# Weight transfers asked for before the row stores land, and the first experts' weight slots refilled by quarters

## What is computed

```python
def hier_moe(u, w_rg, b_rg, w_re, b_re, w_gate, w_up, w_down):
    # top-1 of 4 groups, then top-2 of the 8 experts in that group
    ...
    for e in range(N_EXPERTS):                       # 32
        h = jax.nn.silu(x @ w_gate[e]) * (x @ w_up[e])   # 1024 -> 512
        y = y + cw[:, e:e + 1] * (h @ w_down[e])         # 512 -> 1024
...
h = h + mixer(rmsnorm(h))           # one input projection, short convolution, retention, w_o
h = h + hier_moe(rmsnorm(h))
h = h + (p @ w_ple_proj) * sigmoid(rmsnorm(h) @ w_ple_gate);  y = rmsnorm(h)
```

## Time and profile before

| | |
|---|---|
| median of three runs | 840.43 us |
| the profiled execution | 840.24 us |
| its span | 838.4 us (1.8 us lie around it) |
| TensorE busy | 736.6 us (88%) |
| VectorE, ScalarE, GpSimd busy | 279.1, 180.9, 101.8 us |
| DMA queue q1 | 27248 packets, 237.17 MB, 68.9% of 16 engines' span |
| chain that ended last | TensorE 49%, DMA 34%, VectorE 6% |

### The profile page before, as it was taken

One profiled execution on the slowest core, in us unless ns is written; L12 is line 12 of the kernel. 1 busy time (PEld: TensorE's weight loads), 2 busy tenths in 40 slices (PEclk: granted clock), 3 DMA queues, 4 the chain that ended last, 5 costly groups with the idle time before them and its releaser, 6 DMA issues.

```text
span 838.4 us, 11322 instructions
## 1 busy us (share of the span) xinstructions
PE 736.6 (88%) x4530; PEld 459.6 (55%) x4530; DVE 279.1 (33%) x498; ACT 180.9 (22%) x278; POOL 101.8 (12%) x159
## 2 busy tenths in 40 slices
PE   8999999999999888989999887777777777778996
PEld 7988899989999823333333322222222222226675
DVE  5554578576431632011010100100100100104875
ACT  7242321223331300011111110000000000004576
POOL 0500000000010212211212121121121121110000
PEclk9999999999999989999999999999999999999998
DMA  9541216451763789999999999999999999996301
GB/s 347 227 178 51 75 64 227 176 210 72 295 222 102 281 319 421 418 428 424 425 425 427 424 427 424 426 427 426 426 428 426 428 426 426 426 427 239 151 27 75
DMA packets 36280, 257.30 MB, mean 307 GB/s; under 512 B 7860, under 2 KB 8420, under 8 KB 22792
## 3 DMA queue, kind: packets, MB, share of 16 engines
q1 hardware_dynamic: 27248, 237.17, 68.9%
q0 software_dynamic: 6896, 18.00, 5.7%
q10 hardware_dynamic: 2096, 1.55, 0.6%
HBM read 249.96 MB, written 15.13 MB: 316 GB/s over the span
## 4 chain that ended last, share of the span: by engine, by line
PE 49%; DMA 34%; DVE 6%; ACT 2%; issue 2%; DVEq 0%; SPq 0%; POOLq 0%; ACTq 0%
DMA arena<-in_w_exp 32%; PE ps L1547 19%; PE ps L1739 15%; PE ps L1756 5%; PE ps L1870 3%; PE ps L1590 1%; DVE xh L1410 1%; PE ps L1665 1%; PE ps L1688 1%; PE ps L1655 1%; DMA region_u<-h_rows,index 1%; DVE region_u L1363 1%; DMA y_rows<-region_v,scol 1%; PE ps L1747 1%; PE ps L1626 0%
## 5 line engine op out<-in xcount | busy, mean ns | idle before, releaser
L1739 PE MATMUL ps<-arena,region_u 128*64 128x512 f32 x960 | 219.2, 602 | 46.2 <-DMA arena<-in_w_exp 45.2
L1739 PEld LDWEIGHTS ps<-arena,region_u 128*64 128x64 f32 x960 | 67.0, 138 | 196.1 <-issue 124.7
L1359 DVE SCALAR_TENSOR_TENSOR region_u<-ps,small,region_u 128x256 f32<-128x256 f32 x32 | 15.5, 484 | 376.6 <-ACT region_u L855 376.6
L1547 PE MATMUL ps<-u_hi,w_hi 128*128 128x260 f32 x448 | 129.8, 290 | 4.6 <-issue 2.3
L1547 PE MATMUL ps<-u_lo,w_hi 128*128 128x260 f32 x448 | 127.3, 284 | 0.0
L1547 PE MATMUL ps<-u_hi,w_low 128*128 128x260 f32 x448 | 127.2, 284 | 0.0
L1756 PE MATMUL ps<-arena,region_u 128*64 128x512 f32 x480 | 109.6, 598 | 6.0 <-DMA arena<-in_w_exp 2.5
L1547 PEld LDWEIGHTS ps<-u_hi,w_hi 128*128 128x128 f32 x448 | 85.1, 190 | 6.5 <-issue 3.9
L1547 PEld LDWEIGHTS ps<-u_hi,w_low 128*128 128x128 f32 x448 | 85.2, 190 | 0.0
L1547 PEld LDWEIGHTS ps<-u_lo,w_hi 128*128 128x128 f32 x448 | 85.0, 190 | 0.2
L676 POOL DMA_INDIRECT y_rows<-region_v,scol x32 | 33.4, 1044 | 367.0 <-ACT region_v L859 367.0
(11 more groups left out here) (275 smaller groups left out, 867.9 us busy)
## 6 DMA issues: line engine op xcount, KB each, us to landing
arena<-in_w_exp SPq DMA_DIRECT2D x88, 2048.0 KB, 26.9
arena<-in_w_in SPq DMA_DIRECT2D x35, 512.0 KB, 3.8
region_q<-in_w_exp SPq DMA_DIRECT2D x24, 256.0 KB, 10.2
arena<-in_w_exp SPq DMA_DIRECT2D x8, 512.0 KB, 4.1
arena<-in_w_ple_gate SPq DMA_DIRECT2D x2, 2048.0 KB, 23.6
region_u<-in_xt SPq DMA_DIRECT2D x2, 1040.0 KB, 6.2
arena<-in_state_ret POOLq DMA_DIRECT2D x2, 1024.0 KB, 8.5
xh<-v_few POOLq DMA_DIRECT2D x1, 2048.0 KB, 9.1
```

Of the source, the lines that this page charges most:

```text
L1359: V.scalar_tensor_tensor(hs[b], ps[:, 2 + b, 256:512], rs[b], sg[b], ALU.mult, ALU.mult).then_inc(out_sem, 1)
L1547: last = mm(halves(out)[:, half, :], w[:, k, :], u[:, cols], start=(k == 0 and s == 0), stop=(k == KD - 1 and s == 2))
L1739: last = mm(ps[side * 64:side * 64 + 64, 2 + b, :], xv[:, k // 4, k % 4, :], rows(k % 4 * 2 + side), start=(k == 0), stop=(k == KD - 1))
```

## The change

Three edits in SyncE's program and two in TensorE's increments.

- Spare 1's two patches of 1536 columns are cut into six of 512 (`in_pieces`), so that spare 1 has eight transfers in place of four, in the first filling and in that with unit 16.
- The waits for `h_stored` and `xg_loaded[0]` go. Spare 1 and the first three patches of spare 2 are asked for straight behind spare 0's last patch. The other five patches, which overwrite `part_logit` and the end of `region_u`, wait for `lg_ready` (VectorE, L1343 of the kernel before) and for the job `tp` 7.
- Units 9 to 12, the first four that refill a ring slot, come in quarters of 1024 columns. A new semaphore `piece_used` counts the quarters that expert 0 and the first half of expert 1 have used, and SyncE asks for a quarter as soon as it is free.
- `fills` and `pair_fill` adapt the counts on which TensorE waits. No matmul is added, removed or moved.

```diff
-PIECE_SLOTS = (0, 1)
+PIECED = (3, 4, 9, 10, 11, 12)
...
-                 [(region_v[:, 1024:2560], (0, 1536)), (region_m[:, spare_m + 512:spare_m + 2048], (1536, 3072))]
+                 in_pieces(region_v[:, 1024:2560], 0) + in_pieces(region_m[:, spare_m + 512:spare_m + 2048], 1536)
...
-            sp.wait_ge(h_stored, 16 * 2 * len(STORES))
-            for n in range(4):
+            for n in range(8):
                 load_spare(1, n)
-            sp.wait_ge(xg_loaded[0], 16)
-            for n in range(8):
+            for n in range(3):
+                load_spare(2, n)
+
+            sp.wait_ge(lg_ready, 1)
+            sp.wait_ge(pe_jobs, HEAD.pe(("tp", KD - 1)))
+            for n in range(3, 8):
                 load_spare(2, n)
...
-            for j in range(3):
-                sp.wait_ge(used[j], 1)
-                load_unit(9 + j, PAIR_SLOTS[j])
-            for j in range(3):
-                sp.wait_ge(used[j], 2)
-                load_unit(12 + j, PAIR_SLOTS[3 + j])
+            for unit in range(9, 15):
+                slot = PAIR_SLOTS[unit - 9]
+                for n in range(PIECES if unit in PIECED else 0):
+                    if n < PIECES - 1:
+                        sp.wait_ge(piece_used, (unit - 9) * (PIECES - 1) + n + 1)
+                    else:
+                        sp.wait_ge(used[unit % 3], unit // 3 - 2)
+                    load_piece(unit, slot, n)
+                if unit not in PIECED:
+                    sp.wait_ge(used[unit % 3], unit // 3 - 2)
+                    load_unit(unit, slot)
...
+                    elif k < pieces and k < KD - 1:
+                        last.then_inc(piece_used, 1)
...
+                    if q < pieces:
+                        last.then_inc(piece_used, 1)
...
-                    gate_up(b, units, gu_done, gu_half)
+                    gate_up(b, units, gu_done, gu_half, (KD, PIECES)[b] if first else 0)
...
-                    down(b, rows, down_done)
+                    down(b, rows, down_done, PIECES - 1 if first and b == 0 else 0)
```

More of the change, by code:

```diff
@@ L346, in in_q, with in_pieces @@
             return region_q[:, 96 + n * 512:608 + n * 512]
+        def in_pieces(ap, c0):
+            return [(ap[:, n * 512:n * 512 + 512], (c0 + n * 512, c0 + n * 512 + 512)) for n in range(ap.shape[1] // 512)]
         spare = [[(region_d[:, 0:2048], (0, 2048))] + [(in_q(4 + n), (2048 + n * 512, 2560 + n * 512)) for n in range(3)]
                  + [(region_m[:, spare_m:spare_m + 512], (3584, 4096))],
-                 [(region_v[:, 1024:2560], (0, 1536)), (region_m[:, spare_m + 512:spare_m + 2048], (1536, 3072))]
+                 in_pieces(region_v[:, 1024:2560], 0) + in_pieces(region_m[:, spare_m + 512:spare_m + 2048], 1536)
                  + [(in_q(7 + n), (3072 + n * 512, 3584 + n * 512)) for n in range(2)],
@@ L404, in build @@
         out_stored = [sem(f"out_stored{i}") for i in range(2)]
-        gu_half = sem("gu_half")
+        gu_half, piece_used = sem("gu_half"), sem("piece_used")
         xt_done, xgT_ready, gu_done, silu_done = sem("xt_done"), sem("xgT_ready"), sem("gu_done"), sem("silu_done")
@@ L423, in chunk_wait, with fills @@
             eng.wait_ge(chunk_loaded[n % WIN_SLOTS], 16 * (n // WIN_SLOTS + int(n % WIN_SLOTS > 0)))
+        def fills(unit, slot):
+            return sum(16 * PIECES if n in PIECED else 16 for n in range(unit + 1) if EARLY_SLOTS[n // 6][n % 6] == slot)
         def pair_fill(i, j):
@@ L428, in pair_fill @@
             if isinstance(i, int) and i < 3:
-                turn = sum(slot in slots for slots in EARLY_SLOTS[:i + 1])
-                return slot, 16 * turn + (16 * (PIECES - 1) if slot in PIECE_SLOTS else 0)
-            return slot, i * 16 + (16 * (PIECES - 1) if slot in PIECE_SLOTS else 0)
+                return slot, fills(i * 6 + j, slot)
+            return slot, i * 16 + (fills(17, slot) - 2 * 16)
         w_pp = region_z[:, 0:2 * D]
@@ L1729, in in_spare, with gate_up @@
                 return rows
-            def gate_up(b, units, out_sem, half_sem=None):
+            def gate_up(b, units, out_sem, half_sem=None, pieces=0):
                 xv = xgT[b].rearrange("p (k h r) -> p h k r", h=2, r=ROWS)
@@ L1748, in hidden_t, with down @@
                 last.then_inc(out_sem, 1)
-            def down(b, rows, out_sem):
+            def down(b, rows, out_sem, pieces=0):
                 for q in range(4):
```

## The result

| | before | after |
|---|---|---|
| median of 20 runs each | 838.99 us | 842.36 us |
| lowest, highest | 836.63, 843.0 | 838.49, 843.81 |
| ratio after to before (95%) | | 1.0033 (1.002 to 1.0046) |
| the profiled execution, its span | 840.24, 838.4 | 843.81, 841.8 |

The change costs 0.33%, or 2.8 us (1.7 to 3.9); the two medians lie 3.4 us apart. The forecast of 840.3 us was no change, and a small and certain loss came.

What follows compares the result with a forecast made beforehand. It took the DMA stream of weights to bound the kernel, so only bytes moved in earlier idle or slow stretches pay. Quarters -3.4, finer rows +0.7 and late gather +2.8 gave +0.1 on 840.24: 840.3 us, range 834.5 to 844.5.

Steps and rivals of the forecast that it cites:

- The bound: Weight stream: from 303 us a transfer always waits, so starting the refills a microsecond sooner ends the kernel a microsecond sooner.
- The delay of the gather, +2.8: Before expert 0: without the holds, row stores share engines with patches, so the gather is issued 2.8 us late.
- The turns: Row stores beside patches: two queues with work waiting share an engine by taking turns, one packet each.
- the gather itself I leave at 5.95 us: First expert's rows: the gather, issued late, would still take 5.95 us, running beside the last patches.
- Rival 4: Before the first gate/up: gather 3 us shorter, TensorE's clock stays up, kernel at 832.0 us; chance 0.04.
- The quarters, -3.4: First ring refill: unit 9's fourth quarter lands at 306.9 us, where the whole unit landed at 310.3; gain 3.4 us.
- +0.7 for finer rows: Smaller rows move slower: 0.4 us for units 9 to 12, 0.3 us for spare 1's patches with unit 16.
- They keep the lead: Units 10 to 12, also in quarters, find the queue no longer empty and add nothing to unit 9's lead.
- a rival that carried it to all of units 9 to 16: Quarters and unit 16's patches flow at 250 GB/s: +16.7 us, 857 us; chance 0.03.
- The sum: Whole kernel: quarters -3.4, finer rows +0.7, late gather +2.8 make +0.1 us, hence 840.3 us.
- Rival 2: Row stores queue up behind all patches asked for before them: gather 4.9 us late, 842.4 us; chance 0.15.
- The check named in the prediction: Prediction wrong if the gather is issued by 288.5 us or the 303 to 325 us rate falls well below 402 GB/s.

Runs made afterwards that it cites:

- e6: Changed kernel with the second half of ScalarE's factor rows stored early from other data, so half as many small rows compete; one run, 839.98 us.
- e8: Changed kernel with spare 1's patches uncut (rows of 6 KB in place of 2 KB); ratio to the kernel before 1.0034.
- e4: Kernel before with only spare 1's two large patches cut into six, holds and whole units kept; ratio to the kernel before 1.0022.
- e10: Changed kernel with units 9 to 12 in halves of 1 MB in place of quarters; ratio to the kernel before 1.0024.
- e2: Changed kernel with the quarters taken back: holds off, patches cut, units 9 to 12 whole; ratio to the kernel before 1.0042.
- e9: Kernel before with spare 1's first patch, uncut, asked for ahead of the hold on the row stores; ratio to the kernel before 0.9996.
- e1: Kernel before with units 9 to 12 in quarters, both holds and uncut patches kept; ratio to the kernel before 0.9986.
- e5: Changed kernel with the four factor-row stores issued by SyncE in q1 ahead of the eleven patches, not by ScalarE; ratio to the kernel before 1.0005.
- e11: Changed kernel with the hold on the row stores put back and spare 1's patches uncut; ratio to the kernel before 0.9987.
- e12: Kernel before with spare 1's first patch ahead of the row-store hold, the gather's hold off, units 9 to 12 in halves; ratio to the kernel before 1.0007.
- e3: Changed kernel with the hold on the row stores put back ahead of spare 1; ratio to the kernel before 1.0004.
- e7: Kernel before with cut patches, three of spare 1's asked for ahead of the hold on the row stores; ratio to the kernel before 1.0038.

## Why the prediction was wrong

**The bound: right.** From 440 us on the DMA share and rate are the same, and the stage's end moved with the start of the stream.

**The delay of the gather, +2.8: the right place and sign; the size by luck, from two errors that cancel.** The turns were right (the earlier trace rows against the earlier trace rows was the right choice; 792 to 780 after, and e6 and e8). The rule of the Trainium skill quoted there ("DMA: Bandwidth & Descriptors", "Queues, rings and completion order"), by which 9 to 17 small rows could pass in one turn, isn't borne out by these rows. But the gather was issued 5.03 us late, not 2.8: the estimate let the small rows begin to pass at 281.2, 2.8 us after the first store, as when q1 was running empty. They began after 4.3 us, which is 1.5 of the missing 2.2, and from there needed 9.3 us to land (283.7 to 293.01) in place of 8.6. GpSimd's stores slow down too. The first of them took 7.7 us to land in place of 5.4, by the issues of after from 279.3 to 280.2 us:

```profile
h_rows<-xh POOLq DMA_DIRECT2D x1, 512.0 KB, 7.7
```

And the step "the gather itself I leave at 5.95 us" failed: issued late, it found the patches nearly through and took 3.62. 5.03 - 2.33 and 0.28 of steps between make 2.98 at the first gate/up, against 2.8 forecast. Rival 4's thought, a gather that is quicker without patches beside it, was sound; only its start was late.

**The quarters, -3.4, with +0.7 for finer rows: this is the step that failed.** The forecast -2.7 came out as -1.0. The step is the landing of unit 9's fourth quarter. The sum let it land 4.7 us after it was asked for (4.1 from the earlier trace rows, 0.3 for the rest of the third quarter, 0.3 for a gather), and it took 6.7. The first quarter, asked for at 301.84, did land after 4.2. Those that follow it into the same queue took longer each time, 5.1, then 5.4 for the third (asked for at 305.25) and 6.7 for the fourth (306.43):

```profile
arena<-in_w_exp SPq DMA_DIRECT2D x1, 512.0 KB, 5.4
...
arena<-in_w_exp SPq DMA_DIRECT2D x1, 512.0 KB, 6.7
```

It was also asked for 6.61 us after the first gate/up matmul, where the forecast had 6.36, since the clock came back later. So unit 9 is in at 13.3 us behind that matmul, where before took 14.5 (310.3 - 295.82) and the forecast was 11.1: a gain of 1.2 in place of 3.4. "They keep the lead" held in the main: units 10, 11 and 12 are in 1.2, 0.9 and 0.8 us sooner than before, and the stage has 0.96.

What was wrong in the reasoning is that it took the 4.1 us of the earlier trace rows for the fourth of four, with 0.3 for the third ahead of it. When the fourth was asked for, the third was still 4.2 us from landing (310.65 - 306.43), and from 306 to 310 us the quarters moved at 236 and 254 GB/s, where 418 was assumed. I had the row for it, 244 GB/s for small pieces alone, and used it for a rival that carried it to all of units 9 to 16 and had a chance of 0.03. The right use was in between: slow for the first eight microseconds (that rival's sum has a slip as well: by its own terms it reaches 1% from about 312 GB/s down, not 295). The Trainium skill's rule of at least 1 MiB a transfer ("DMA: Bandwidth & Descriptors", "Rules for kernel authors") agrees with the trace in an empty queue, 410 and 434 GB/s for whole units, 401 to 303 for halves and 236 to 313 for quarters, and not in a full one, 419 for quarters. Why the engines stand at share 0.70 from 306 to 308, with two to four quarters asked for and not landed, stays open. The +0.7 for finer rows no run here shows by itself; e4, which has a part of it alone, is at 1.0022.

**The sum.** +2.98 and -0.96 are the stage's +2.02 (by construction), and that is inside the timed 1.7 to 3.9. The forecast had 2.8 - 2.7 = +0.1. Rival 2 named the time that came (842.4), with another mechanism: stores served behind all patches, gather at 293. The gather did come at 294.04, or 293.02 without the head's 1.02, and the stores did enter 1.4 us late; but e6 and e8 show that the small rows wait by turns.

**The check named in the prediction.** "If the rate from 303 to 325 us falls well below 402" was the test that would show the prediction wrong, and it did show it: 350 GB/s, and still 373 from 307 to 324, the like stretch behind a first matmul that is 4.0 us later.

## What to carry to other kernels

A hold in a queue of large transfers may be there to let another queue's many small rows pass: before it is removed, count those rows and price each at one turn of the large row. Refilling in pieces: a unit counts when its last piece is in, and the time that one piece alone takes to land (4.2 us here) is the price of the first piece only; the fourth took 6.7. Read that landing before anything else. A change of a few microseconds here is below what one profile of each can tell, since the granted clock moves the head by 1 to 1.5 us from execution to execution.

## What the hardware showed that I had not expected

- Two queues with work took turns row by row whatever the sizes: 792 rows of 2 KB to 780 of 64 bytes, so that 0.05 MB took 4 us beside 1.45 MB. With patches asked for ahead of them, the small rows first passed 4.3 to 4.7 us after their store was issued, in place of 2.9.
- The same transfer of 512 KB landed after 4.2 us as the first into an empty queue, and after 5.1, 5.4 and 6.7 as the second, third and fourth.
- The same gather of the first experts' rows took 3.21 to 3.91 us with the weights' queue running down (e8, e10, e2, after, e9) and 5.9 to 7.0 beside patches (before, e1, e5, e11, e12, e3); e4, e6 and e7 lie between (4.8 to 5.5).
- The granted clock fell to the lower level (1.2 GHz) for some microseconds in the middle of gapless TensorE work, in other places in other executions of the same head: a mean of 0.57 over 277 to 281 us in e1, 0.64 over 252 to 254 in before, where e2 has 1.00 from 250 to 260.
